# Small TensorE operations of the mixers placed one at a time between the k steps of the next piece

## The reference, cut to what matters

```python
s = jnp.einsum('bnqgrd,bnkgd->bngrqk', qb, kb).astype(jnp.float32) * scale + bias      # kind A
p = jax.nn.softmax(jnp.concatenate([s, sink_l], axis=-1), axis=-1)[..., :-1]
o = jnp.einsum('bngrqk,bnkgd->bnqgrd', p.astype(v.dtype), vb)
```

## Time and profile before

| | |
|---|---|
| median of 3 runs | 3634.64 us |
| the profiled execution | 3637.97 us, span 3636.0 us |
| busy: TensorE, weight loads, VectorE, ScalarE | 91%, 88%, 64%, 39% |
| mean granted clock of TensorE | 0.954 of full |
| read from HBM | 677.47 MB, 189 GB/s over the span |

### The profile page before, as it was taken

How to read it: one execution, slowest core, us unless ns; L and a number is a source line. 1 busy time by engine, 2 the same in 40 slices (tenths; PEclk the granted TensorE clock), 3 DMA queues, 4 the chain that set the end, 5 groups by cost and what they waited for, 6 DMA issues and landing times.

```text
span 3636.0 us, 63711 instructions
## 1 busy us (share of the span) xinstructions
PE 3309.7 (91%) x27198; PEld 3201.8 (88%) x27198; DVE 2310.5 (64%) x2566; ACT 1404.1 (39%) x1376; POOL 158.3 (4%) x292
## 2 busy tenths in 40 slices
PE   3386997899999987988999999998898999999997
PEld 2386887899999987877899999998887899999997
DVE  6777678765656666566755555556556755555555
ACT  1133333344444433344443334334344533343343
POOL 2111101200000000001000000000001000000000
PEclk7698998999999998999999999999999999999999
DMA  9677766855555553333455555554333455555553
GB/s 319 225 269 271 259 209 253 280 195 188 195 196 189 192 173 116 121 109 125 157 193 189 195 196 189 192 196 152 119 113 122 147 173 196 193 191 193 196 190 123
DMA packets 320589, 681.68 MB, mean 187 GB/s; under 512 B 14608, under 2 KB 21460, under 8 KB 320004
## 3 DMA queue, kind: packets, MB, share of 16 engines
q1 hardware_dynamic: 283440, 560.11, 46.1%
q0 software_dynamic: 31232, 109.07, 8.6%
q10 hardware_dynamic: 5780, 10.53, 0.9%
HBM read 677.47 MB, written 7.94 MB: 189 GB/s over the span
## 4 chain that ended last, share of the span: by engine, by line
PE 80%; DVE 11%; DMA 5%; issue 3%; ACT 2%; ACTq 0%; POOLq 0%; POOL 0%; DVEq 0%; SPq 0%
PE G L594 47%; PE Dn L594 32%; DMA ada_raw<-in_w_ada 3%; DVE w_lo L1045 2%; DVE ada_acc L1146 2%; DMA raw<-in_w_in 2%; PE Dn L597 1%; DVE sq L1081 1%; ACT w_hi L1773 1%; DVE negmax L1373 0%; DVE xT L1400 0%; DMA raw<-in_w_ffn_up 0%; DVE xT L1611 0%; DVE h_lo L1619 0%; DVE s_sb L1343 0%
## 5 line engine op out<-in xcount | busy, mean ns | idle before, releaser
L594 PE MATMUL G<-h_hi,w_hi 128*128 128x256 f32 x5760 | 1634.8, 284 | 60.7 <-DVE w_lo L1045 24.4
L594 PE MATMUL G<-h_lo,w_hi 128*128 128x256 f32 x5760 | 1619.1, 281 | 0.0
L594 PE MATMUL G<-h_hi,w_lo 128*128 128x256 f32 x5760 | 1617.8, 281 | 0.0
L1773 ACT CAST w_hi<-raw 128x2048 fp32r<-128x2048 f32 (+2 forms) x536 | 1016.9, 1899 | 1529.0 <-DMA raw<-in_w_down 429.8
L1045 DVE TENSOR_TENSOR w_lo<-raw,w_hi 128x2048 fp32r<-128x2048 f32 (+2 forms) x536 | 1219.1, 2275 | 610.0 <-ACT w_hi L1773 607.7
L594 PEld LDWEIGHTS G<-h_hi,w_hi 128*128 128x128 f32 x5760 | 1107.3, 192 | 75.4 <-issue 29.4
L594 PEld LDWEIGHTS G<-h_lo,w_hi 128*128 128x128 f32 x5760 | 1106.9, 192 | 0.7
L594 PEld LDWEIGHTS G<-h_hi,w_lo 128*128 128x128 f32 x5760 | 1106.3, 192 | 0.0
L594 PE MATMUL Dn<-act_hi,w_hi 128*128 128x256 f32 x2752 | 760.0, 276 | 7.3 <-DVE act_lo L1482 7.3
L594 PE MATMUL Dn<-act_lo,w_hi 128*128 128x256 f32 x2752 | 759.7, 276 | 0.0
L594 PE MATMUL Dn<-act_hi,w_lo 128*128 128x256 f32 x2752 | 759.7, 276 | 0.0
(11 more groups left out here) (195 smaller groups left out, 1613.2 us busy)
## 6 DMA issues: line engine op xcount, KB each, us to landing
raw<-in_w_up SPq DMA_DIRECT2D x128, 1024.0 KB, 5.4
raw<-in_w_down SPq DMA_DIRECT2D x128, 1024.0 KB, 5.0
ada_raw<-in_w_ada POOLq DMA_DIRECT2D x192, 512.0 KB, 5.7
raw<-in_w_in SPq DMA_DIRECT2D x88, 1024.0 KB, 5.3
raw<-in_w_ffn_gate SPq DMA_DIRECT2D x44, 1024.0 KB, 5.0
raw<-in_w_ffn_up SPq DMA_DIRECT2D x44, 1024.0 KB, 4.9
raw<-in_w_ffn_down SPq DMA_DIRECT2D x44, 1024.0 KB, 5.0
raw<-in_w_o SPq DMA_DIRECT2D x32, 1024.0 KB, 5.1
```

What stands on the lines that cost most here:

```text
L594: return nc.tensor.matmul(o, lhsT, rhs, start=start, stop=stop, skip_group_check=True)
L1773: s.copy(w_hi[j][:, 0:PIECE_K * n], raw[j][:, 0:PIECE_K * n]).then_inc(hi_done, 1)
```

## The change

TensorE's hook table is keyed by k steps in place of pieces. `piece` gets an argument `p` and runs the hooks of place 4p+kk behind its k step kk. `hook(p, ...)` counts the items of a slot: the first goes behind the first k step of piece p+1, the second behind the second, the third behind the third, and the fourth and all later ones behind the fourth. The former functions are cut into items: `slot` becomes `hook_slot`, with one item for each `finish`, each `scores`, and one for the products with V (`outputs`); the gates, pool maps and value transposes become one item for each use of MISC. pe_done is still incremented by the last matmul of the last k step, ahead of the items there. On VectorE and ScalarE the hooks `group_lo` and `group_hi` are registered earlier, so that they stand at the head of their slot; nothing else changes on them, nor on SyncE and GpSimd.

```diff
-            def piece(quad, j, out, rhs_hi, rhs_lo, kts, first, last, n=PIECE_N, tiles=None, misc_tile=False):
+            def piece(quad, j, out, rhs_hi, rhs_lo, kts, first, last, n=PIECE_N, tiles=None, misc_tile=False, p=None):
...
-                i.then_inc(pe_done, 1)
+                    if kk == PIECE_K - 1:
+                        i.then_inc(pe_done, 1)
+                    if p is not None:
+                        run_hooks(PIECE_K * p + kk)
...
             hooks = {}
+            in_slot = collections.Counter()
 
             def hook(p, fn, *args):
-                hooks.setdefault(p, []).append((fn, args))
-
-            def run_hooks(p):
-                for fn, args in hooks.pop(p, []):
+
+                kk = min(in_slot[p], PIECE_K - 1)
+                in_slot[p] += 1
+                hooks.setdefault(PIECE_K * (p + 1) + kk, []).append((fn, args))
+
+            def run_hooks(at):
+                for fn, args in hooks.pop(at, []):
                     fn(*args)
...
-            def slot(done, new, base):
+            def outputs(done, base):
+                misc_open(out_name(done), mbase[0])
+                for H, kind, h in done:
+                    i = finish(H, kind, h, base + H, 1)
+                i.then_inc(misc_w, 1)
+
+            def hook_slot(p, done, new, base):
 
                 for n in range(max(len(done), len(new))):
                     if n < len(done):
                         H, kind, h = done[n]
-                        finish(H, kind, h, base + H, 0)
+                        hook(p, finish, H, kind, h, base + H, 0)
                     if n < len(new):
                         H, kind, h = new[n]
-                        scores(H, kind, h, base + H)
+                        hook(p, scores, H, kind, h, base + H)
                 if done:
-                    misc_open(out_name(done), mbase[0])
-                    for H, kind, h in done:
-                        i = finish(H, kind, h, base + H, 1)
-                    i.then_inc(misc_w, 1)
+                    hook(p, outputs, done, base)
...
             for b in range(4):
-                hook(9 + b, lru_gates, b)
-            hook(22, pool_map)
-            hook(18, v_turn1, [0, 1])
-            hook(19, v_turn1, [2, 3])
-            hook(23, v_turn1, [4, 5])
-            hook(24, v_turn1, [6, 7])
+                hook(9 + b, lru_gate, b, "r", lru_wa)
+                hook(9 + b, lru_gate, b, "i", lru_wi)
+            for g in range(4):
+                hook(22, pool_map, g)
+            for v, p in enumerate((18, 18, 19, 19, 23, 23, 24, 24)):
+                hook(p, v_turn1, v)
...
                     for p, ts, evac in V_TURN_AT:
-                        hook(p, v_turn, ts, evac)
+                        for v in ts:
+                            hook(p, v_turn, v, evac)
...
-                            piece(lq + g, j, G[b], h_hi, h_lo, 4 * j, j == 0, j == 3, n, tiles)
-                            run_hooks(4 * g + j)
+                            piece(lq + g, j, G[b], h_hi, h_lo, 4 * j, j == 0, j == 3, n, tiles, p=4 * g + j)
```

More of the change, by code:

```diff
@@ L704, in f_columns, with v_turn1 @@
                 i.then_inc(misc_w, 1)
[L706 to L711, removed]
-                    i.then_inc(misc_w, 1)
+            def v_turn1(v):
+                pe.wait_ge(z_evac, 4 if v < 4 else 5)
+                misc_open(f"v{v}")
+                for t in range(QT):
+                    i = turn(MISC[:, t * P:(t + 1) * P], zT[:, Z_V + v, t * P:(t + 1) * P])
+                i.then_inc(misc_w, 1)
             def finish(H, kind, h, no, part):
@@ L814, in _ @@
                             pe.wait_ge(g_free[b], use)
-                        piece(idx // 4, idx % 4, G[b], h_hi, h_lo, k0, i == 0, i == 1)
-                        run_hooks(idx)
+                        piece(idx // 4, idx % 4, G[b], h_hi, h_lo, k0, i == 0, i == 1, p=idx)
             if stage >= 2:
@@ L831, in gate_up @@
                                 pe.wait_ge(g_free[b], i + base)
-                            piece(quad + b, j, G[b], h_hi, h_lo, 4 * j, j == 0, j == 3)
-                            if static is not None:
-                                run_hooks(MIX1_PIECES + static + 4 * b + j)
+                            piece(quad + b, j, G[b], h_hi, h_lo, 4 * j, j == 0, j == 3,
+                                  p=None if static is None else MIX1_PIECES + static + 4 * b + j)
                 def down(quad, i, dbase, first=False):
@@ L873, in _, with v_turn @@
                     zc = l * Z2_EVACS + 9
-                    def v_turn(ts, evac):
+                    def v_turn(v, evac):
                         pe.wait_ge(z_evac, zc + evac)
[L877 to L881, removed]
+                        misc_open(f"val{v}", base)
+                        for t in range(QT):
+                            i = turn(MISC[:, t * P:(t + 1) * P], zT[:, v, t * P:(t + 1) * P])
+                        i.then_inc(misc_w, 1)
                     def swapped(src):
@@ L919, in _ @@
                     for p, (done, new) in SLOTS2.items():
-                        hook(p, slot, done, new, l * HEADS2 + HEADS1)
+                        hook_slot(p, done, new, l * HEADS2 + HEADS1)
                     for b_, p in enumerate(QK_SS_AT):
@@ L962, in _ @@
                             pe.wait_ge(g_free[b], gb[b] + (6 + 2 * half + f // 2))
-                            piece(lq + (10 + half), f, G[b], h_hi, h_lo, k0, True, True)
-                            run_hooks(40 + 4 * half + f)
+                            piece(lq + (10 + half), f, G[b], h_hi, h_lo, k0, True, True, p=40 + 4 * half + f)
                     def up2(quad, i, first=False):
@@ L970, in up2 @@
                                 pe.wait_ge(g_free[0], gb[0] + (i + 10))
-                            piece(quad, j, G[0], h_hi, h_lo, 4 * UP_ORDER[j], j == 0, j == 3)
-                            if first:
-                                run_hooks(48 + j)
+                            piece(quad, j, G[0], h_hi, h_lo, 4 * UP_ORDER[j], j == 0, j == 3, p=48 + j if first else None)
                     def down2(quad, i):
@@ L1648, in _ @@
                     hook(4, read_rstd, "mix")
+                    for kind in "CBA":
+                        hook(GROUP_HI_AT[kind], group_lo, kind)
                     for p, (done, new) in SLOTS2.items():
@@ L2139, in _ @@
                         hook(p, squares_l, q)
+                    for kind in "CBA":
+                        hook(GROUP_HI_AT[kind], group_hi, kind)
                     for p, (done, new) in SLOTS2.items():
@@ L2152, in _ @@
                         hook(GROUP_SS_AT[kind], group_square, kind)
-                        hook(GROUP_HI_AT[kind], group_hi, kind)
                     for p in range(48):
```

27 lines of the change are left out of this document (12 added, 15 removed).

## The result

The changed kernel takes 3829.52 us (median of 4 runs, 3826.43 to 3837.34) against 3634.54 us before: ratio 1.0544, 95% interval 1.0523 to 1.0566. That is slower by 195 us; the forecast was 190.

The account below looks back on a forecast made before the run. TensorE was taken to hold 80% of the chain of waits, nearly all in piece matmuls. Layers +77, first mixer -7, restarts +10 and clock +110 give +190 us on 3634.64: 3825 us, own range 3760 to 3890.

Parts of the forecast that it names:

- The loop: Layers' mixers: product with V, copy, w_hi, w_lo, normalising, next transposes; 5.4 us chain left with 1.4 or 2.8 us cover.
- The size of the uncovered chain: Layers' mixer slots: period becomes work plus 5.4 us, 14.0 with two heads, 10.9 with one; +54.4 us a layer.
- +77: Both layers' mixers: 54.4 us a layer from chained slots less 16 gained, net +38.4 a layer.
- extra link of the first norm sum: Layers' mixers: a norm sum with its Newton steps adds 4.3 us in the first such slot.
- The clock: Layers' and first mixers: clock falls behind 44 waits at 2.5 us each, +110 us (bounds 0 and 229).
- Restarts, +10: Large matmul behind a small one takes 0.1 us longer; some 130 more such changes, +10 us (bounds 0 and 20).
- First mixer, -7 and 15 for its six falls: First stage's mixer: eight heads' chain and saved waits, net -7 us; six of the 44 clock falls, 2.5 us each.
- What is gained, 16 us a layer: Layers' mixers: waits outside the chained slots covered by k steps, 16 us with their clock (bounds 0 and 20).
- 3.0 for a boundary: Layers' mixers, boundary from slot 21 to 22: +3.0 us by the chained slots' terms.
- The clock holds: Rival, mixers: only the structure counts, without the 110 us of clock: 3715 us; chance 0.22.
- The clock stays low: Rival, mixer loops: clock low throughout, 264 us in place of 110: 3980 us; chance 0.17.
- Faster: Rival, between product with V and next transposes: waits within a bunch are the bound, 70 us gained, 3565; chance 0.06.

Follow-up runs that it names:

- e3: Changed kernel, but in nine slots of each layer ScalarE copies the product's result behind w_hi of the piece three ahead: 3754.36 us, ratio 1.0341.
- e4: Changed kernel, but the heads' operations stand in two places only, behind the next piece's first and second k steps: 3719.73 us, ratio 1.0239.
- e6: As e4, but broadcasts, rotations and norm sums of these slots also behind the second k step (except slot 30's value transpose): 3656.65 us, ratio 1.007.
- e5: Changed kernel, but each slot's small operations in a row behind the next piece's first k step (slot 30's value transpose behind its fourth): 3613.15 us, ratio 0.9952.
- e9: Changed kernel with 14 to 50 additional constant transposes ahead of 19 slots' transposes in each layer, sized to their waits: 3737.29 us, ratio 1.0286.
- e1: Change made in the first stage's mixer alone, both layers and the two moved hooks as in the kernel before: 3636.47 us, ratio 1.001.
- e10: Changed kernel, but head slots' operations in a row behind the next piece's first k step (one slot 30 transpose excepted), head-free slots spread: 3579.76 us, ratio 0.9857.
- e7: Changed kernel, but head slots in a row at their piece's end as before, only head-free slots spread, two hooks put back: 3604.02 us, ratio 0.9926.

## Why the prediction was right

It gave 3825 us and 3829.52 was measured. Its steps:

- *The loop.* Right. The chain from product to transposes is 5.3 us (5.4 forecast), 19 slots of a layer wait (19), 70.5 us in layer one and 70.7 in layer two, where "some 120 us or more in all" was said. e3 takes the first link out and the wait falls; e4, e6 and e5 lengthen the cover by k steps and the waits fall in that order.
- *The size of the uncovered chain.* The clock is out of the way in e9, so its slot starts can be held against the periods that were worked out (layer one, us; a stretch runs from the first transposes of one slot to those of the other):

| slots | before | forecast | e9 | changed |
|---|---|---|---|---|
| 14 to 17 | 32.1 | 41.0 | 41.1 | 46.4 |
| 22 to 27 | 55.4 | 71.1 | 73.2 | 80.8 |
| 29 to 32 | 41.2 | 38.4 | 40.8 | 43.5 |
| 32 to 40 | 78.8 | 108.4 | 111.1 | 132.9 |

  Each is within 2.7 us, and the period of a two-head slot is 14.0 as it stood. Over the whole of a layer's mixer e9 is 53.8 and 46.9 us above before, where the sum had 38.4 and its share of the restarts. So +77 should have been +101, or some more, since in layer two e9's clock is better than that of the kernel before. (The extra link of the first norm sum adds up to 4.2 us from its terms, where 4.3 is written; nothing hangs on it.)
- *The clock.* Forecast: 2.5 us for each fall, 95 us for the 38 of the two layers. Measured: 92 us between the changed kernel and e9, 2.4 us for each wait. This was a middle between two prices of the trace of before, and that it hit so well is in part luck. e3 gave back 21 us of clock by shortening some seven waits of layer one, 3 us for each. And not every wait has a fall of its own: by the clock's records 22 stretches of each layer are at the lower level in the changed kernel, 6 and 2 in e9, 7 and 7 in the kernel before.
- *Restarts, +10.* Not seen. With the clock restored TensorE's own busy time in layer one is that of before within 3 us, although it changes between large and small matmuls more often. The large matmul behind a small one does take 0.1 us longer, but it starts before the small one has ended (in the kernel before 0.39 us from 1572.10, with the product ending at 1572.17).
- *First mixer, -7 and 15 for its six falls.* Measured: a ratio of 1.001 in e1, 0 to 7 us by its interval; a single trace cannot tell it, since the same first stage is 4 us ahead in one and 3 us behind in another. The net of +8 was too high by some 1 to 8 us, or 12 by the trace after.
- *What is gained, 16 us a layer.* Other waits than those for s_sb fell by 12.4 in layer one. But e9's layers as wholes are only 5 and 8 us better than their chained stretches alone (53.8 against 58.7 us over before, 46.9 against 55.0), where the forecast had 13: its 16 less 3.0 for a boundary.
- So that the sum was only 5 us off is luck too, since errors cancel: the structure of the layers was too small by 24, and restarts, clock and first mixer together too large by about as much.
- *The rivals.* "The clock holds" (3715) is 22 us under what e9 measures, 3737, where the clock is made to hold; it did not by itself. "The clock stays low" would have needed 264 us of clock. The rule of the Trainium skill that was weighed with it (TensorE: Matmul & The Clock Gate, "Loop structure matters more than you think") is that the loop nest decides whether matmuls stay warm, and its bad case is a long wait for a load in each turn. The waits here are shorter and for another engine; the trace agrees with the rule all the same: the granted clock is 0.75 and 0.80 in slots that each hold a wait of 3.7 us, and 1.00 in the dense feed-forward loop. "Faster" had its point of decision right, a chain of 2.8 us or 1.4, but the chain is 5.3.
- *What the prediction did not say* is the general form. It named the product with V as the start of the chain and the ropes and norms as extra links. The expectation of e4 made the same choice and was 30 us off: moving the product forward left waits of 3.2 to 5.7 us, like that of slot 30 behind a broadcast. The place of the last operation that a weight piece's hand-over stands behind is what counts.

One thing is open: e5 and e10 differ from the kernel before in the place of the row and in the two moved hooks together, and which of the two takes away the long wait for h_lo was not tried. (In e7, with the hooks put back and the rows of head slots at the ends of their pieces, it is 3.9 us as before.) By the code, the two can hardly be parted. With the hooks moved and the rows at the ends of their pieces, TensorE's value transpose of slot 30 waits for ScalarE's copy of the swap, which stands behind group_hi, which waits for piece 31, which stands behind that transpose. With the rows moved and the hooks left, piece 32 waits for h_lo, which stands on VectorE behind row maxima of scores that stand inside piece 32.

## What to carry to other kernels

Before small operations are spread between large ones, look for a chain that leaves one group of them, passes through engines that also prepare the large ones' operands, and comes back to the next group: it has the whole distance between the groups as its cover, and spreading a group shortens that distance by as much as it spreads. Moved as a block, with the two hooks, the same operations cost nothing inside a piece and gained 0.5%; spread only where nothing of the next group depends on them, they gained another 0.9%. And count the last reader, not the best-known one: an order on VectorE or ScalarE makes each operation of the slot a link.

## What had not been expected of the hardware

- More work, less time: 621 transposes of a constant in each layer, put where TensorE would stand idle for 1.7 to 5.7 us, took 92 us off (3829.5 to 3737.3). They bring the granted clock from 0.87 and 0.86 to 0.97 and 0.99; from slot 24 to slot 27 of layer one (1569.2 to 1611.0 in e9), whose three periods each hold a row of 32 such transposes and nothing else in place of the wait, it is 1.00. Here transposes keep the clock up. A transpose of 128 by 128 took 0.114 us in a row of 32.
- The lower level costs nearly as much as the waits themselves: of the 94.7 us that layer one lost, 52 are idle time and 42 are the same instructions at the lower level. In e3, 17 us less waiting brought 21 us less busy time in layer one.
